# Trunk step on one core: exponentials, scaling and row maxima reordered in the last eight blocks of prompt attention

## The reference, cut to what matters

```python
def _sparse_attend(q, ks, vs, valid):
    qg = q.reshape(B, Q, N_KV_HEADS, GQA_GROUP, HEAD_DIM)
    s = jnp.einsum('bqhgd,bqnhd->bqhgn', qg, ks).astype(jnp.float32) * (HEAD_DIM ** -0.5)
    s = jnp.where(valid[:, :, None, None, :], s, -jnp.inf)
    p = jax.nn.softmax(s, axis=-1).astype(vs.dtype)
    o = jnp.einsum('bqhgn,bqnhd->bqhgd', p, vs)
    return o.reshape(B, Q, N_HEADS * HEAD_DIM)
```

## Time and profile before

| | |
|---|---|
| time, three runs | 1847.68 us median (1846.29 to 1847.91) |
| the profiled execution | 1845.26 us, span 1843.5 us |
| share of the span in which PE is busy | 97% |
| DVE, ACT, POOL busy | 79%, 51%, 23% |
| prompt attention of blocks 8 to 15 (PE's first transposes of each) | 608.48 to 652.46 us |
| first product with the gathered values | 663.51 us |

### The profile page before, as it was taken

The page is one execution under the profiler, slowest core; times in us unless marked ns, Lnnn a source line. Parts: engine busy times, 40 slices in busy tenths (PEclk is TensorE's granted clock), DMA queues, the critical chain, the costliest instruction groups (busy, mean ns, idle before and its releaser), DMA issues.

```text
span 1843.5 us, 35847 instructions
## 1 busy us (share of the span) xinstructions
PE 1781.1 (97%) x14078; PEld 1698.7 (92%) x14078; DVE 1455.6 (79%) x2188; ACT 932.3 (51%) x1464; POOL 420.8 (23%) x312
## 2 busy tenths in 40 slices
PE   7999999999999798999999999999999899999997
PEld 7999999987965488999999989999999799999996
DVE  5988887676978537988887599888876998887875
ACT  4555562353357736555562375555523575556333
POOL 3000044262220536000043230000542320002430
PEclk9999999999999999999999999999999999999998
DMA  5653423236110232343323323343324123433231
GB/s 162 202 192 100 114 87 103 87 100 146 49 54 1 67 117 70 92 114 100 105 92 98 109 70 107 99 114 98 103 81 120 52 63 104 114 105 101 82 103 47
DMA packets 275472, 180.73 MB, mean 98 GB/s; under 512 B 9366, under 2 KB 271902, under 8 KB 274845
## 3 DMA queue, kind: packets, MB, share of 16 engines
q1 hardware_dynamic: 266071, 158.50, 30.1%
q0 software_dynamic: 2144, 13.04, 2.0%
q10 hardware_dynamic: 7150, 7.70, 1.7%
HBM read 169.56 MB, written 8.08 MB: 96 GB/s over the span
## 4 chain that ended last, share of the span: by engine, by line
PE 75%; DVE 15%; ACT 6%; issue 3%; DMA 1%; POOL 0%; SPq 0%; ACTq 0%; DVEq 0%; POOLq 0%
PE ps L1372 41%; PE ps L1251 15%; PE ps L1435 9%; PE ps L1495 2%; DVE w_lo L1960 2%; PE ps L1715 2%; DVE q_lo L2647 1%; ACT xf L752 1%; ACT xh L750 1%; PE ps L1500 1%; ACT p_t L887 1%; DVE w_lo L2540 1%; PE ps L1272 1%; DVE q_sum L2724 1%; DVE xf L2010 1%
## 5 line engine op out<-in xcount | busy, mean ns | idle before, releaser
L2811 POOL TENSOR_TENSOR hl<-hid_all,hh 128x520 fp32r<-128x520 f32 x56 | 98.1, 1784 | 750.4 <-ACT hh L1111 750.4
L1041 ACT CAST w_hi<-w_sum 128x1024 fp32r<-128x1024 f32 x160 | 167.9, 1050 | 114.8 <-DVE w_sum L2522 107.3
L2540 DVE TENSOR_TENSOR w_lo<-w_sum,w_hi 128x1024 fp32r<-128x1024 f32 x160 | 194.8, 1219 | 4.5 <-ACT w_hi L1041 4.5
L1251 PE MATMUL ps<-hh,w_hi 128*128 128x260 f32 x896 | 191.7, 284 | 2.0 <-DVE w_lo L1960 2.0
L1251 PE MATMUL ps<-hh,w_lo 128*128 128x260 f32 x896 | 189.1, 282 | 0.0
L1372 PE MATMUL ps<-t_hi,w_hi 128*128 128x260 f32 x640 | 161.5, 284 | 0.7 <-DVE w_lo L2540 0.3
L1372 PE MATMUL ps<-xh,w_hi 128*128 128x260 f32 x640 | 159.9, 282 | 0.9 <-DVE w_lo L2540 0.9
L1372 PE MATMUL ps<-t_hi,w_lo 128*128 128x260 f32 x640 | 160.6, 283 | 0.0
L1372 PE MATMUL ps<-xh,w_lo 128*128 128x260 f32 x640 | 159.5, 283 | 0.0
L1251 PEld LDWEIGHTS ps<-hh,w_hi 128*128 128x128 f32 x896 | 145.4, 188 | 3.0 <-issue 2.7
L1251 PEld LDWEIGHTS ps<-hh,w_lo 128*128 128x128 f32 x896 | 145.6, 188 | 0.2
(11 more groups left out here) (376 smaller groups left out, 5256.9 us busy)
## 6 DMA issues: line engine op xcount, KB each, us to landing
w_raw<-in_ffn_wi_dram SPq DMA_DIRECT2D x176, 512.0 KB
w_raw<-in_ffn_wo_dram SPq DMA_DIRECT2D x16, 1024.0 KB
w_raw<-in_ffn_wo_dram SPq DMA_DIRECT2D x32, 512.0 KB
w_raw<-in_ffn_wo_dram SPq DMA_DIRECT2D x16, 768.0 KB
w_raw<-in_attn_w_in_dram SPq DMA_DIRECT2D x8, 1024.0 KB
keys_scratch<-key_half POOLq DMA_DIRECT2D x2, 2048.0 KB, 8.7
w_raw<-in_attn_w_o_dram SPq DMA_DIRECT2D x4, 1024.0 KB
x_in<-in_x_prompt_dram ACTq DMA_DIRECT2D x4, 512.0 KB, 9.7
```

Of the source, the lines that this page charges most:

```text
L1041: nc.scalar.copy(blocks(st, j)[1][0][:, x], w_sum[:, c % 2, x]).then_inc(s_sums_hi, 1)
L1251: mm = nc.tensor.matmul(ps[0:mc, bank + 2 * m + h, 0:HT], w[:, k, m, 0:mc], x(k)[:, h * HT:(h + 1) * HT], start=first and k == 0 and w is ...
L2540: nc.vector.tensor_tensor(lo[:, x], w_sum[:, (st.chunk + j) % 2, x], hi[:, x].bitcast(F32), ALU.subtract).then_inc(s_sums_lo, 1)
L2811: nc.gpsimd.tensor_tensor(hl[:, k, :], hid_all[:, k, :], hh[:, k, :].bitcast(F32), ALU.subtract).then_inc(s_hl, 1)
```

## The change

For blocks 8 to 15 (`SHORT` = `SCALED` = 8):

- ACT's `normalised` is left out. DVE scales the four rows in one TENSOR_TENSOR with the reciprocal spread along each row, directly behind the reciprocal, and this raises `s_p` by two.
- In DVE's iteration B the order was reciprocal(B-1), low part(B-3), maxima(B, 0), maxima(B, 1). It becomes maxima(B, 0), reciprocal and scaling(B-1), maxima(B, 1), low part(B-3).
- In ACT's iteration B both pairs of exponentials now stand ahead of the copies of block B-1; before, the second pair stood behind the first two copies. From block 12 on `out_high(B-2)` stands ahead of the copy `sample_keys(2*(B-LATE))`.
- POOL no longer waits for `s_rinv` ahead of the gathers; it still waits for the indices (`s_idx`) and for the two small loads (`s_newkv`).

```diff
+        SHORT = LATE - N_KV
+        SCALED = SHORT
...
                         exponentials(B, 0)
+                        if B >= SHORT:
+                            exponentials(B, 1)
                         if B > LATE:
                             sample_keys(2 * (B - LATE) - 1)
                         probs_out(B - 1, 0)
-                        exponentials(B, 1)
+                        if B < SHORT:
+                            exponentials(B, 1)
                         probs_out(B - 1, 1)
+                    if B >= 2:
+                        out_high(B - 2)
                     if B >= LATE:
                         sample_keys(2 * (B - LATE))
-                    if B >= 2:
-                        out_high(B - 2)
-                    normalised(B)
+                    if B < SCALED:
+                        normalised(B)
...
-                    if B > 1:
+                    if 1 < B < SHORT:
                         inverse(B - 1)
-                    if B >= 3:
+                    if 3 <= B < SHORT:
                         out_low(B - 3)
                     if B >= 2:
                         dve.wait_ge(s_tp, tile_base[B - 1])
                     row_maxima(B, 0)
+                    if B >= SHORT:
+                        inverse(B - 1)
...
                     row_maxima(B, 1)
+                    if B >= SHORT:
+                        out_low(B - 3)
...
             def inverse(B):
                 dve.wait_ge(s_exp, B + 1)
-                nc.vector.reciprocal(row_inv[:, B % 2, :], row_sum[:, B % 2, :]).then_inc(s_rinv, 1)
+                x = nc.vector.reciprocal(row_inv[:, B % 2, :], row_sum[:, B % 2, :])
+                if B < SCALED:
+                    x.then_inc(s_rinv, 1)
+                else:
+                    n = (BLOCKS[B][0] + 1) * P
+                    rows = (sc if B < LATE else sc_late)[:, 1 - B % 2, :, 0:n]
+                    done(step(x))
+                    nc.vector.tensor_tensor(rows, rows, row_inv[:, B % 2, :].unsqueeze(2).broadcast_to([P, 4, n]), ALU.mult).then_inc(s_p, 2)
...
-                    pool.wait_ge(s_rinv, B + 1)
+                    if B < SHORT:
+                        pool.wait_ge(s_rinv, B + 1)
```

## The result

| | before | after |
|---|---|---|
| median of 20 runs | 1846.88 us (1845.23 to 1848.85) | 1849.51 us (1847.47 to 1853.00) |
| ratio of after to before | | 1.0014, 95% interval 1.0008 to 1.0020 |
| the profiled execution | 1845.26 us | 1853.0 us, span 1850.8 us |

The change costs 0.14%, some 2.6 us. The interval is all on the slower side, though the size is inside the 0.2% that the prediction calls no change. The forecast was a gain of 2.5 us, a ratio of 0.9987, and 1849.51 lies 1.3 us above the end of its range. Traces start at different moments; where two are compared, starts are counted from PE's first transposes of block 7, at 598.35 before and 599.48 after.

What follows compares the result with a forecast made beforehand. TensorE bounds the kernel, an engine-to-engine chain blocks 12 to 15. PE alone gains 5.1 - 0.5 = 4.6 us, but gathers 3.3 late allow 2.5: 1847.68 - 2.5 = 1845.2 us, range 1841.8 to 1848.2.

Steps and rivals of the forecast that it cites:

- The loop and its cut: Blocks 8 to 15: first maxima no longer wait for exponentials; seven rounds shrink from 42.4 to 37.3 us as written out.
- the rival of twice that: DVE's scalings take 2.3 and 1.2 us, gathers land at 667.0, and the kernel is slower at 1851.2 us; chance 0.06.
- The rival in which PE gains little: The scaling-maxima-exponentials-copies chain holds every round near 5.9 us; gain 0 to 1.5, 1847 us; chance 0.12.
- The rival without holding: Scalings do not hold POOL's gathers, which end at 657.2, so PE's whole 4.6 us arrives: 1843.1 us; chance 0.27.
- 0.5 + 2.4 + 0.6 - 0.9: Lateness of the last gather: slots' start, holds by scalings, hold by `w_lo`, quicker landing; 2.6 us by averages, 3.3 taken.
- start of the slots: Ahead of `hot_val` the 1.22 us scaling comes in and the low part of 0.4 goes: slots and gathers 0.5 us later.
- holds by scalings: Gathers issued inside the seven scalings of blocks 9 to 15 wait for their end: 2.4 us together, 2.95 as written out.
- holds by `w_lo`, more than before: The 2.29 us `w_lo` operation always catches one gather: 0.6 us more than before, 1.1 as written out.
- landing: The last gather lands 2.8 us after issue instead of 3.7, since the two weight loads start earlier: 0.9 us quicker.
- the clock: PE's standstill of some 2 us ahead of the products lowers its clock, costing 1.7 us: 1846.9 us; chance 0.1.
- nothing is lost behind it: Behind the products' start PE's work runs in order, so the 2.5 us gained there stays whole to the end.
- Slack: Before, the last gather landed at 657.6 and PE reached the products at 663.51 without a wait: 5.9 us of slack.

Runs made afterwards that it cites:

- row by row: The changed kernel with four TENSOR_SCALARs, one for each row, in place of the scaling TENSOR_TENSOR: 1.0019 of the kernel before.
- the order alone: The changed kernel's new order, with ScalarE scaling blocks 8 to 15 as before: 0.9971 of the kernel before, 1841.73 us.
- the change from block 12: Order and scaling changed for the last four blocks alone, 12 to 15, against the kernel before: ratio 0.9980.
- products later: The changed kernel with the products of the gathered values moved behind the high part of the second column group: 1.0011 of the kernel before.
- the filler: The changed kernel with 20 identity transposes ahead of the wait for `hot_val` and 36 ahead of the wait for the gathers: 1.0003 of the kernel before.
- block 8's scaling behind `hot_val`: The changed kernel with reciprocal and scaling of block 8 issued behind `hot_val` instead of ahead of it: 1.0009 of the kernel before.
- the scaling alone: The kernel before, in its old order, with DVE instead of ScalarE scaling blocks 8 to 15: 1.0023 of the kernel before.

## Why the prediction went wrong

**Right.** The loop and its cut: rounds 4.7, 5.6, 4.7, 6.2, 5.7, 6.2 and 5.3 us against the written 4.8, 5.7, 4.5, 6.2, 5.2, 6.1 and 4.8; gain 5.6 for 5.1. The cost of the scaling, with the operand spread along the row:

```profile
L2386 DVE TENSOR_TENSOR sc<-sc,row_inv x4: 1224/1224/1225, 603.6 to 624.4; 128x1024 f32<-128x1024 f32 x4
L2386 DVE TENSOR_TENSOR sc_late<-sc_late,row_inv x4: 692/692/693, 629.1 to 644.8; 128x512 f32<-128x512 f32 x4
```

1.22 and 0.69 us, as costed, so the rival of twice that falls. The rival in which PE gains little falls by the rounds: PE gained 5.6 us in them and 3.7 up to the products, where I had 4.6: the rounds gave 0.5 more than written and the start of the slots, below, took 1.5 more. The place of the new end, PE at the products behind a DMA into `v_sel`, was right too, and its cause: gathers held by DVE's two-operand operations. The rival without holding fell with five long gathers beside scalings in the changed kernel and none row by row. That rival was the inferred sentence of the Trainium skill, SBUF — State Buffer, section Who interferes with whom, by which `tensor_tensor` does not stall such DMAs; the runs decide against it for gathers. They agree with the other sentence of that section of the Trainium skill, that two SBUF inputs contend with GpSimd's reads of SBUF.

**The step that failed: the gathers late by "0.5 + 2.4 + 0.6 - 0.9", of which I took 3.3.** The last landed 7.8 us late. Term by term, measured in the profiled execution:

| term | predicted | measured |
|---|---|---|
| start of the slots | 0.5 | 1.96 |
| holds by scalings | 2.4 to 2.95 | 1.9 |
| holds by `w_lo`, more than before | 0.6 to 1.1 | 2.4 |
| landing | -0.9 | +1.5 |
| sum | 2.6 to 3.6, taken 3.3 | 7.8 |

*Start.* DVE's `hot_val` was late by 604.74 - 603.09 - 1.13 = 0.5, as counted. But PE's standstill ahead of the slots was then 2.53 us (before 1.41), and they took 3.47 us instead of 2.03. I had put the clock only at the products.

*`w_lo`.* I let this stage catch one gather. There are two such operations; before, the second came after the last gather. With gathers later and PE earlier the two overlap, and holds of 1.91 and 1.54 us stand against 1.03 before.

*Landing.* I took 2.8 us, since the weight loads start earlier. But the second `w_lo` frees the buffer for one more load of 1 MB, and the late gathers now land beside that one: 5.2 us. `w_lo` and landing are one oversight, a collision behind PE's old arrival, and they come together: with the order alone, and with the change from block 12, the last gather was issued ahead of `w_lo` and PE did not wait at all.

*What of this is firm.* Four kernels issue the last gather 2.5 us behind the end of the second `w_lo`, beside the same load: the changed one, products later, the filler, and block 8's scaling behind `hot_val`. It landed 5.2, 5.0, 3.7 and 3.8 us after its issue. What makes the difference is open. The slots' clock fell in some executions and not in others with the same standstill. With the slots at full clock and a landing of 3.7 us the gathers are 4.95 us late (the filler's trace: +64.20 against a landing at +59.25 before). That is still above the 3.3 that I took, by the hold in `w_lo` and by a landing that got no quicker.

**The second step that failed: "nothing is lost behind it".** I gave the clock a chance of 0.1 and 1.7 us, inside a forecast of a wait of 2 us. The wait was 5.48 us and the products took 3.1 us longer; in the other kernels with a wait of 3.35 us and more they took 1.6 to 2.7 us longer, in one 0.1. So at the end of the products the profiled execution is late by their start, 67.12 - 65.16 = 1.96, and by 3.1, together 5.0 us. The medians differ by 2.6. As an estimate from the traces: an execution with the slots at full clock and a landing of 3.7 us starts the products at +64.20, 1.0 us ahead of before, behind a wait of some 4.1 us. Behind a wait of 4.08 they took 9.76 us, 2.7 longer, so it ends 1.7 us late; 2.6 lies between 1.7 and 5.0. The rest of the traces' 7.7 us lies outside: 1.1 ahead of block 7 and 1.6 behind the products or around the span, where nothing was changed. How often the clock falls at each place over the 20 runs can't be read from one profile.

**Slack.** Gathers with 5.9 us of slack was right (four fewer changed nothing before). PE took 3.7 of it by itself and the gathers' lateness of 7.8 the rest: 5.9 - 3.7 - 7.8 = -5.6, the wait of 5.5. Predicted were 5.9 - 4.6 - 3.3 = -2.0.

## What to carry to other kernels

Slack between two streams that are moved towards each other is spent from both sides: list what each passes on its way, up to beyond the old meeting point, for here the last gather met an operation and a weight load that it had always been ahead of. Moving work to an idle engine is costed by whom its memory accesses hold as well as by its busy time; DVE had room and the scaling was as quick as costed, yet the order alone, with ScalarE left to scale, is 0.29% faster than before and the whole change 0.14% slower. A wait of a few microseconds on PE is costed with the clock behind it.

## What the runs showed of the hardware

- A gather of 128 rows that POOL issues inside a DVE TENSOR_TENSOR with both inputs in SBUF ends 0.9 to 1.0 us after that operation, and takes 1.08 to 2.91 us instead of 1.00. One issued ahead of it is not held: the gather at 655.91 took 1.00, though `w_lo` began at 656.59. Pieces of 512 elements cut 2.91 to 1.32, and TENSOR_SCALARs of some 350 ns did not hold the two gathers issued just inside them (1.10 and 1.00 us).
- The granted clock fell, to 0.50 in the changed kernel, behind standstills of PE of 3.35 to 5.48 us (products of 8.67 to 10.15 us instead of 7.07) and behind some of 2.4 to 2.5 us (slots of 3.06 to 3.47 us instead of 2.03), but not behind others of 2.53 us, nor behind 3.40 us in one kernel (7.15 us). It fell behind 1.89 and 1.94 us in the rounds of the kernel with the scaling alone (0.72 over 6 us each; transposes of 1.97 us instead of 1.09), but not behind 1.98 there. Behind 1.1 to 1.4 us ahead of the slots it did not fall.
- The last gather landed 3.7 to 5.2 us after its issue in four kernels, beside a 1 MB weight load issued 2.5 us ahead of it (DMA share 0.99 in the changed kernel); 2.8 was the median without weight loads.
